# The doubling of a block inverse: GpSimd's mask, ScalarE's copy and VectorE's sums for all eight heads in one instruction, instead of one per half

## The reference

```python
def step(state, inp):
    r_t, w_t, k_t, v_t, kk_t, a_t = inp
    sa = jnp.einsum('bhij,bhj->bhi', state, -kk_t)
    state = (state * w_t[:, :, None, :]
             + sa[..., None] * (kk_t * a_t)[:, :, None, :]
             + v_t[..., None] * k_t[:, :, None, :])
    return state, jnp.einsum('bhij,bhj->bhi', state, r_t)
```

## Time and profile before

| what | value |
|---|---|
| median of 3 runs | 5868.87 us (5862.19 to 5869.34) |
| profiled execution, device time | 5872.54 us |
| its span, first to last instruction | 5871.0 us |
| TensorE busy | 4976.8 us, 85% of the span |
| VectorE busy | 3036.8 us, 52% |
| ScalarE busy | 1971.4 us, 34% |
| GpSimd busy | 586.9 us, 10% |
| mean granted TensorE clock | 0.917 of full speed |
| GpSimd's mask (L430) | 224 instructions, 380.4 us |

### The profile page before, as it was taken

How to read it: one execution, slowest core, us unless ns; L and a number is a source line. 1 busy time by engine, 2 the same in 40 slices (tenths; PEclk the granted TensorE clock), 3 DMA queues, 4 the chain that set the end, 5 groups by cost and what they waited for, 6 DMA issues and landing times. The chain is left out here.

```text
span 5871.0 us, 75990 instructions
## 1 busy us (share of the span) xinstructions
PE 4976.8 (85%) x26088; PEld 3775.8 (64%) x26089; DVE 3036.8 (52%) x5631; ACT 1971.4 (34%) x3047; POOL 586.9 (10%) x535
## 2 busy tenths in 40 slices
PE   7999999998999778888888888599628888888577
PEld 5878878887877664444444444488527777777465
DVE  3555555565666336666555555444126534455565
ACT  3322332323322114444333333110316444355233
POOL 0112211121222110000000000000020000000010
PEclk9999999999999869999999999899659999999888
DMA  4323222322221200000000000333337645568422
GB/s 128 105 79 92 81 67 68 102 80 61 65 65 50 69 13 10 8 6 8 4 6 6 4 4 4 131 107 100 105 111 269 253 183 186 211 254 300 148 103 75
DMA packets 423694, 545.88 MB, mean 93 GB/s; under 512 B 37808, under 2 KB 282928, under 8 KB 422688
## 3 DMA queue, kind: packets, MB, share of 16 engines
q1 hardware_dynamic: 377600, 436.10, 22.8%
q0 software_dynamic: 19072, 59.86, 2.9%
q10 hardware_dynamic: 26784, 46.93, 2.1%
HBM read 432.74 MB, written 110.08 MB: 92 GB/s over the span
## 5 line engine op out<-in xcount | busy, mean ns | idle before, releaser
L458 PE MATMUL fr_fb<-fr_hT_h,fr_w_h 128*128 128x512 f32 (+1 forms) x1312 | 527.4, 402 | 16.6 <-DVEq L991 10.8
L430 POOL TENSOR_TENSOR fr_Lm<-fr_M,fr_join 128x512 f32<-128x512 f32 x224 | 380.4, 1715 | 1588.9 <-DVE fr_M L1030 975.0
L458 PE MATMUL fr_fb<-fr_hT_r,fr_w_h 128*128 128x512 f32 (+1 forms) x1312 | 526.0, 401 | 0.0
L458 PE MATMUL fr_fb<-fr_hT_h,fr_w_r 128*128 128x512 f32 (+1 forms) x1312 | 525.3, 400 | 0.0
L1478 PEld LDWEIGHTS aq_t_bank<-at_ident,aq_sc 128*128 128x128 f32 x1920 | 215.2, 145 | 369.2 <-issue 310.5
L842 DVE TENSOR_TENSOR fr_w_r<-fr_w_raw,fr_w_h 128x1024 fp32r<-128x1024 f32 (+1 forms) x164 | 209.5, 1278 | 430.0 <-ACT fr_w_h L673 429.7
L133 PE MATMUL ex_yps<-ex_down_w,ex_hidT 128*128 128x512 f32 x1176 | 328.1, 441 | 121.0 <-DVE ex_hidT L2382 121.0
L1557 ACT COPY aq_pt<-aq_t_bank 128x512 f32<-128x512 f32 x320 | 187.1, 585 | 577.0 <-PE aq_t_bank L1478 576.5
L133 PEld LDWEIGHTS ex_yps<-ex_down_w,ex_hidT 128*128 128x128 f32 x1176 | 247.9, 214 | 191.4 <-issue 124.5
L1508 PE MATMUL aq_o_bank<-aq_pt,at_vs 128*64 128x512 f32 x640 | 359.5, 653 | 0.9 <-DVE aq_pt L1723 0.9
L1528 ACT ACTIVATE aq_sc<-aq_sc,aq_ust 128x640 f32<-128x640 f32 (+4 forms) x260 | 283.9, 1092 | 166.7 <-DVE aq_ust L1672 158.8
(11 more groups left out here) (450 smaller groups left out, 10361.4 us busy)
## 6 DMA issues: line engine op xcount, KB each, us to landing
ex_raw<-in_w_exp_gate_up SPq DMA_DIRECT2D x64, 2048.0 KB, 10.6
fr_w_raw<-in_w_in SPq DMA_DIRECT2D x160, 512.0 KB, 3.8
ex_raw<-in_w_exp_down SPq DMA_DIRECT2D x32, 2048.0 KB, 12.1
s_z<-fr_zs SPq DMA_DIRECT2D x160, 256.0 KB
s_rows<-ex_y ACTq DMA_DIRECT2D x49, 512.0 KB, 7.1
mx_mg<-s_z SPq DMA_DIRECT2D x16, 1024.0 KB, 7.8
fr_zc<-s_z SPq DMA_DIRECT2D x15, 903.0 KB, 6.8
fr_x_t<-in_x SPq DMA_DIRECT2D x16, 512.0 KB, 5.0
```

The lines of the kernel that those rows point to most:

```text
L430: pool.tensor_tensor(Lm[:, g, :, :], M[:, 4 * g:4 * g + 4, 0, :], join[:, lev:lev + 1, :].to_broadcast([P, HG, CH]), ALU.mult).then_inc(l_ ...
L458: ins = pe.matmul(bank[0:cols_, :], (w_h, w_h, w_r)[p][:, k, c, 0:cols_].bitcast(F32R), (hT_h, hT_r, hT_h)[p][:, c, :].bitcast(F32R), star ...
```

## The change

In each level the mask, the copy of `X` and the sums are one instruction over 8 heads (128x1024) where there were two over 4 heads (128x512). The semaphores keep their counts: one instruction adds 2, and it waits for what the second half waited for. TensorE's program is not touched; its waits for "half g" are on counts that now come in steps of two.

```diff
@@ gpsimd
                 for lev in range(LEVELS):
-                    for g in range(2):
-                        if lev == 0:
-                            pool.wait_ge(m_ok, 8 * c + 4 * g + 4)
-                            if c:
-                                pool.wait_ge(x_made, 12 * (c - 1) + 11 + g)
-                        elif lev == 1:
-                            pool.wait_ge(l0_made, 2 * c + g + 1)
-                            pool.wait_ge(e_ok, 14 * c + g + 1)
-                        else:
-                            pool.wait_ge(x_made, 12 * c + 2 * (lev - 2) + g + 1)
-                        pool.tensor_tensor(Lm[:, g, :, :], M[:, 4 * g:4 * g + 4, 0, :],
-                                           join[:, lev:lev + 1, :].to_broadcast([P, HG, CH]), ALU.mult).then_inc(l_ok, 1)
+                    if lev == 0:
+                        pool.wait_ge(m_ok, 8 * c + 8)
+                        if c:
+                            pool.wait_ge(x_made, 12 * c)
+                    elif lev == 1:
+                        pool.wait_ge(l0_made, 2 * c + 2)
+                        pool.wait_ge(e_ok, 14 * c + 2)
+                    else:
+                        pool.wait_ge(x_made, 12 * c + 2 * (lev - 1))
+                    pool.tensor_tensor(Lm[:, :, :, :].rearrange("p g h t -> p (g h) t"), M[:, :, 0, :],
+                                       join[:, lev:lev + 1, :].to_broadcast([P, H, CH]), ALU.mult).then_inc(l_ok, 2)
@@ scalar
-                    for g in range(2):
-                        act.wait_ge(x_made, 12 * c + 2 * (lev - 1) + g + 1)
-                        if c or lev > 1:
-                            act.wait_ge(e_made, 12 * c + 2 * (lev - 2) + g + 1)
-                        act.copy(flat(X[:, g, :, :]), xb[:, g, :]).then_inc(x_ok, 1)
+                    act.wait_ge(x_made, 12 * c + 2 * lev)
+                    if c or lev > 1:
+                        act.wait_ge(e_made, 12 * c + 2 * (lev - 1))
+                    act.copy(X[:, :, :, :].rearrange("p g h t -> p g (h t)"), xb[:, :, :]).then_inc(x_ok, 2)
@@ vector
-                for g in range(2):
-                    dve.wait_ge(l_ok, 14 * c + g + 1)
-                    dve.tensor_tensor(invT[:, g, :, :], Lm[:, g, :, :], eye, ALU.add).then_inc(e_ok, 1)
-                    dve.wait_ge(l0_made, 2 * c + g + 1)
-                    dve.tensor_tensor(inv[:, g, :, :], by4(xb[:, g, :]), eye, ALU.add).then_inc(d_ok, 1)
+                dve.wait_ge(l_ok, 14 * c + 2)
+                dve.tensor_tensor(all8(invT), all8(Lm), eye, ALU.add).then_inc(e_ok, 2)
+                dve.wait_ge(l0_made, 2 * c + 2)
+                dve.tensor_tensor(all8(inv), both_banks(xb), eye, ALU.add).then_inc(d_ok, 2)
...
-                    for g in range(2):
-                        dve.wait_ge(e_made, 12 * c + 2 * (lev - 1) + g + 1)
-                        dve.wait_ge(d_ok, 12 * c + 2 * (lev - 1) + g + 1)
-                        dve.wait_ge(e_ok, 14 * c + 2 * (lev - 1) + g + 1)
-                        if lev < LEVELS - 1:
-                            dve.tensor_tensor(inv[:, g, :, :], by4(xb[:, g, :]), inv[:, g, :, :], ALU.add).then_inc(d_ok, 1)
-                        dve.tensor_tensor(invT[:, g, :, :], by4(eb[:, g, :]), invT[:, g, :, :], ALU.add).then_inc(e_ok, 1)
+                    dve.wait_ge(e_made, 12 * c + 2 * lev)
+                    dve.wait_ge(d_ok, 12 * c + 2 * lev)
+                    dve.wait_ge(e_ok, 14 * c + 2 * lev)
+                    if lev < LEVELS - 1:
+                        dve.tensor_tensor(all8(inv), both_banks(xb), all8(inv), ALU.add).then_inc(d_ok, 2)
+                    dve.tensor_tensor(all8(invT), both_banks(eb), all8(invT), ALU.add).then_inc(e_ok, 2)
```

More of the change, by code:

```diff
@@ L1013, in _ @@
             slot()
-            eye = ident[:, :].rearrange("p (o t) -> p o t", o=1).to_broadcast([P, HG, CH])
+            eye = ident[:, :].rearrange("p (o t) -> p o t", o=1).to_broadcast([P, H, CH])
+            all8 = lambda t: t[:, :, :, :].rearrange("p g h t -> p (g h) t")
+            both_banks = lambda t: t[:, :, :].rearrange("p g (h t) -> p (g h) t", h=HG)
             def chunk(c):
```

## The result

The changed kernel takes 5954.2 us (5940.4 to 5955.7) against 5869.1 us: a ratio of 1.0141, 95% interval 1.0123 to 1.0159, so 85 us slower, where 58 were forecast. The profiled execution of the changed kernel is its fastest, 5940.36 us with a span of 5938.8, so its trace shows 68 us of the 85.

A forecast was written before the change was run, and what follows sets the result against it. TensorE was taken to bound the chunks, busy 1751 of 1844 us. Levels 0 and 1, collisions, the two sums and the clock gave 24 + 16 + 4 + 5 + 9 = 58 us, so 5927 us, range 5893 to 5962.

The forecast's parts named there:

- TensorE's wait before L573 from 8 to some 25 us: Sign to look for in the profile after: TensorE's wait at the level-0 transposes grows from 8 to some 25 us.
- I take ... rounded up to 2.5: GpSimd's mask of 1024 elements: 2 x 1.27 - 0.1, rounded up to 2.5 us.
- Levels 0 and 1, 24 us: Transposes wait for all heads' mask: 14 us in chunks 0 to 10, 10 us in five later chunks.
- Collisions, 16 us: VectorE and the longer GpSimd mask exclude each other: 8 us at `lora`, 8 at `expand` and `gate_lora`.
- over 50: Sign to look for: TensorE's waits before L485 (`lora`) and L513 (`expand`) together go from 40 to over 50 us.
- the rival "Faster": A later single mask lets VectorE's shift finish first, so `lora` and `expand` lose most waits: 5857 us; 4 in 100.
- The sums, 9 us: In chunks 11 to 15, later `inv` costs 4 us at five levels, later `invT` 5 us at `lora` and `expand`.
- `invT` ... ends 1.1 us later: VectorE's second sum ends 1.1 us later, delaying everything VectorE has behind the sums by 1.1 us.
- The clock, 9 us: Eight new long TensorE waits, each followed by slower clock losing 1.7 us; two thirds counted, 9 us.
- 49 + 9 forecast: The forecast's 58 us: terms 24, 16, 4 and 5 for levels 0 and 1, collisions and sums, plus 9 for the clock.

The follow-up runs named there:

- Levels 2 to 6 alone: The kernel before, with only GpSimd's mask merged for eight heads, at levels 2 to 6 alone: 5876.8 us, ratio 1.0013.
- a finer mask: The kernel before, with the second half's mask of level 0 in two pieces of two heads: 5871.7 us, 1.0007; with filled waits 5848.5 us.

## Why the prediction was right or wrong

**Sign, place, mechanism: right.** TensorE stayed the bound, VectorE's saved time was worth nothing, and the largest new wait is where it was said to be. "TensorE's wait before L573 from 8 to some 25 us": 27.8. The chunks 11 to 15 grew by 4.9 to 10.0 us (3 to 6 forecast), 0 to 3 by 0.3 to 2.5, among the least; chunk 10 grew by 8.4. The median is inside the range.

**"I take ... rounded up to 2.5": nearly.** 2.34 to 2.41 undisturbed. The fixed part is about 0.2 us (2 x 1.27 less 2.34), not 0.1.

**Levels 0 and 1, 24 us: nearly right in the changed kernel.** The waits there grew by 21.6. Chunk 1 lost 1.2 for 1.3. In chunk 11 the product of eight heads began 7.15 us after the level-0 mask (1588.28 to 1595.43) for 7.4 by the prediction's steps. By itself the merged mask of these levels costs 35 us: the waits there grow by 28.8 (15.8 to 44.6), as it lacks the joint `invT` that comes early, and the clock makes up about the rest.

**Collisions, 16 us: mechanism right, size too large.** An instruction is held for nearly one mask, and the hold doubled. The Trainium skill ("SBUF — State Buffer", Who interferes with whom) gives the rule of the lock held for a whole instruction; this trace agrees, 1.06 to 2.21 us for the shift, and the sums that read PSUM varied by no more than 18 ns in either kernel. But `lora` and `expand` went from 40 to 47.0 and not "over 50", because the later start of the single mask lets the shift go first in chunks where the half masks had met it. That is the mechanism of the rival "Faster"; it was real, took off part of the 16, and was far from turning the sign. Levels 2 to 6 alone cost 8 us.

**The sums, 9 us: mis-sized, the term that failed.** The product behind `inv` loses time at the five levels of the five chunks that the prediction named, but 0.3 to 0.65 us and not 0.15, so 9.6 us and not 4. "`invT` ... ends 1.1 us later" held (1.06). What was missed is what the 1.1 us runs into. Without the merged mask it uses up the shift's lead of 0.53 us. The joint `invT` of level 0, which had no term of its own, holds back the first mask of level 1, 12.1 us of new waits. And all of it brings time at 1.2 GHz. So the sums alone cost 54 us in place of 9, level 0's 18 and the later ones 45. On top of the mask alone they cost 37 (85 less 48), 18 in the chunks of the profiled executions (66.9 less 48.7). The prediction priced each merge as if the others were fixed; in the runs 48 and 54 make 85. The Trainium skill ("Perfetto Trace Analysis", Optimizing Scalar/DVE Operations) advises grouping for a saturated engine; VectorE, 1042 of 1844 us busy before, was 28 us less busy after (15 forecast), and that bought nothing. The same section says that breaking up instructions may help where ScalarE or VectorE is not saturated and causes bubbles on other engines. VectorE's halves of before against the merged sums agree with that (54 us); the copy on ScalarE, which nobody waited for, made no difference (0.9997).

**The clock, 9 us: mis-sized.** 23 to 27 us by the records of the profiled executions, 14 to 25 by filling the waits. The count was low: it had eight new spells of 1.7 us lost, and chunks 10 and 11 alone have 10.2 and 13.7 us more at 1.2 GHz, up to 12 us lost. That slower fills cover other waits did happen, as in chunk 11 above, but it took off less than the third that the prediction allowed: 23 us are lost of 27.

**The sum.** In the profiled execution waits (with the 7 us inside the products) and clock came to 44 + 23 us for the 49 + 9 forecast: a little too much in the waits, too little in the clock. Within the waits the collisions were put too high and the products too low. That the chunks' 67 lie near the 58 is thus partly luck. Of the 27 us between the forecast and the measured 85, 10 are in the profiled execution, and the other 17 in what its time lacks to the median. The copy cost nothing, as forecast.

**Open.** The three other executions of the changed kernel took 14 us more than the profiled one, at a mean clock of 0.911 in place of 0.915. That points to more time at 1.2 GHz, but no trace shows where. The later sums cost 45 us with 30 of it in the chunks; 14 more lie behind them, in code that is the same in all kernels. There the profiled execution spent 20.5 us more at 1.2 GHz (874.8 in place of 854.3), up to 10 of the 14, but why is open; over all runs this part took 3857 to 3882 us, with 820 to 875 at 1.2 GHz. And which waits bring the lower clock was seen but not predicted from anything.

## What to carry to other kernels

Where TensorE is the bound and other engines feed it in halves, merging the halves on an engine with time to spare saves what nobody waits for and gives up the overlap of a half's work with the next half's. That costs nothing where the consumer comes later anyway, as with the copy; otherwise price it at the consumer, by how much later the last and the first piece arrive. Price merges together as well as one by one, since a start that moves by 1 us decides who is first where two engines exclude each other. And count TensorE's longer waits (here of 2 to 5 us) twice: they cost themselves and often several microseconds at half the clock behind them, so that cheap matmuls in such waits can win more than shortening them.

## What the runs showed of the hardware

A GpSimd multiplication of 128x512 float32 took 1.27 us and one of 128x1024 2.34, almost the whole of it proportional to size. A VectorE instruction with both inputs in SBUF was held for up to nearly a whole one of them (1.1 us, then 2.2), one with an input in PSUM not at all. Filling waits of up to 5 us with matmuls nobody needs made an unchanged program 24 us faster, and the slower one 48. And a finer mask that shortened waits by 5 us won nothing, since 17 us more were spent at 1.2 GHz, partly in chunks whose waits were the same.
